# Two attention sublayers on one core: rotation after the query and key units, softmax over two score buffers, head norm by PSUM bank

## The chip, the cores and the metric

The kernel runs on one core of a Trainium2 chip. The metric is the device time of one execution in microseconds (us), as a median of several. The engines named below are TensorE (PE in the profile, with PEld for its weight loads), VectorE (DVE), ScalarE (ACT), GpSimd (POOL) and SyncE (SP, which issues the weight transfers). Each engine works through its own instructions in program order and waits on semaphores for the others. SBUF is the on-chip memory; PSUM is the accumulator memory that TensorE writes, eight banks of 128 x 512 fp32 values, here P[:, 0] to P[:, 7].

## The reference

One block (a mixer of four branches and a mixture of experts), and behind it two layers of three sublayers each, on 256 rows of 1024 values in fp32. The six sublayers are ffn, sparse attention, ffn, ffn, differential attention, ffn. The change touches the two attention sublayers:

```
# sparse: 16 query heads of 64, one shared key and one value head, an indexer of 8 heads
q, k, qi, ki = rope(...)                      # rotates 16 of each 64 columns
score = sum_h w_h * relu(qi_h . ki)           # the 64 best keys of each row are kept
p = softmax(mask(q . k * 64**-0.5));  o = p v
# differential: 8 heads, two query/key sets, values of 128
a = softmax(q1 . k1) - lambda * softmax(q2 . k2)
o = rmsnorm_over_128(a v) * subln_g * (1 - lam_init)
y = o @ w_out                                 # 1024 x 1024, in both
```

Meanwhile the modulation of the second layer, silu(c) @ ada_w[1], is computed: 1024 x 9216 weights, of which nothing else of the sparse sublayer depends.

## The kernel before

Weights stream through `ring`, six slots of 1 MB. SP issues the load for a slot when the unit that lay in it six units earlier is used up. Weights of a projection or an ffn are split into two fp32r parts, `w_hi` (ACT, `high`, L1470) and `w_lo` (DVE, `low`, L1942), and TensorE multiplies three products of these parts. The output projections (`square_out`, L701) and the modulation (`p_ada`, `fill` in `sparse`) take the ring's fp32 weights directly.

An attention sublayer goes through these stages (PE: `sparse` L1302, `differential` L1379; ACT: `a_sparse` L1824, `a_differential` L1859; DVE: `v_sparse` L2551, `v_differential` L2614).

- `project` (L1291): 7 units of 256 columns (sparse) or 12 (differential), each for both halves i of the rows, 14 or 24 tiles; ACT copies each from bank 0 or 1 to `proj` and counts `proj_out`.
- Rotation (`apply_rope`, L2527, DVE, six instructions a call). DVE waits for the last tile, computes two rows of gains (`out_gain`, `in_gain`) ahead of that wait, rotates everything and then marks `roped`. In the differential sublayer it also waits for an exponential on ACT (`lam_exp`), which stands behind the last copy of `project`.
- `turns` (L1280): PE waits for `roped`, then transposes `proj` in groups of four blocks through banks 2 and 3, and ACT copies each group to `qT`, `kT` or `qiT` (`turned`, L1799).
- In the sparse sublayer the indexer (16 small score tiles, a weighted sum on DVE, and the choice of the 64 best by eight rounds of max and replace), with 36 modulation units given out between the steps of PE by `fill`.
- The softmax loop, n = 0 to 7: row half i = n // 4, heads in four groups hg = n % 4; i = 0 has 128 keys, i = 1 has 256. `scores(n)` writes four score tiles into banks 0 and 1. On DVE `probs_rows` (L2540) waits for them, scales and masks them into the one buffer `big`, takes the row maxima and negates them, then waits for ACT's four exponentials (`softmax_exps`, L1806) and takes the reciprocals; the probabilities go to `pr`. PE transposes `pr` (banks 2, 3), ACT copies that to `pT`, and PE multiplies with the values. PE issues `scores(n+1)` ahead of its wait for the probabilities of n.
- In the differential sublayer the outputs of the eight heads stay in banks 4 to 7. Behind the loop ACT squares all four banks in one instruction, PE sums the squares over each head's 128 values with a matrix of ones into banks 0 to 3, ACT takes Ln and Exp of 128 x 2048 values, and DVE multiplies all in one instruction into `oT`.
- `square_out` writes banks 4 to 7; near its end the first half of the next sublayer's normalized rows is transposed (`turn_normed`, L678) into banks 2 and 3. `turnover` (ACT L1759, DVE L2480) holds the row norms, the residual and the next pre-norm.

## Time and profile before

| | us |
|---|---|
| median of 3 runs (2267.04 to 2272.16) | 2269.96 |
| the profiled execution: its time | 2268.83 |
| its span (first to last instruction) | 2267.1 |

Positions in the trace are us from the start of the span. The sparse sublayer's projection ends at about 1308, its output projection starts at 1424; in the differential sublayer it is 1937 and 2029. A row of the timeline has the start, the busy time, the engine, the line, the operation with its shapes and count, and in brackets how long the engine had been idle and what released it. A fp32 matmul shows as two instructions. TensorE's clock has two levels, 1.2 and 2.4 GHz; the profile gives it as a mean granted clock, 0.50 and 1.00 for the two.

### The profile page before, as it was taken

The page shows a single profiled execution, that of the slowest core. Times are in us where ns is not written, and L with a number is a line of the kernel's source. Part 1 is how long each engine was busy: PE and PEld are TensorE (multiplying, and loading weights), DVE is VectorE, ACT ScalarE, POOL GpSimd, SP SyncE. Part 2 cuts the span into 40 slices and gives each one's busy share as a digit, 9 for nine tenths or more (in the row PEclk, how much of TensorE's full clock was granted, in tenths as well). Part 3 has the DMA queues.
Part 4 walks back from the last instruction along what each step waited for, and adds up shares of the span by engine and source line. Part 5 has one row for each costly group of instructions (what it writes and reads, how often), then busy time and mean ns, then how long its engine had stood idle before and what let it go on. Part 6 is the DMA issues. An engine that isn't in the chain of part 4 may idle for free.

```text
span 2267.1 us, 29656 instructions
## 1 busy us (share of the span) xinstructions
PE 2102.3 (93%) x12013; PEld 1752.0 (77%) x12013; DVE 1189.9 (52%) x1691; ACT 889.3 (39%) x1277; POOL 61.0 (3%) x144
## 2 busy tenths in 40 slices
PE   8999989989899999997999967899999999559998
PEld 6777778778478877876999922599989999437998
DVE  2060352431278888887645554355565554334554
ACT  1233411111156677674433424343343434334333
POOL 5000000000000000000000000000000000000000
PEclk9999986979989999998999998899999999669999
DMA  7875230304689898895555698355546565103562
GB/s 226 286 244 184 75 112 1 112 1 149 264 325 339 295 339 315 299 346 189 178 193 167 205 368 319 112 186 183 188 150 218 172 202 187 56 9 122 186 197 100
DMA packets 207240, 441.81 MB, mean 195 GB/s; under 512 B 8108, under 2 KB 158732, under 8 KB 183584
## 3 DMA queue, kind: packets, MB, share of 16 engines
q1 hardware_dynamic: 201568, 424.70, 54.0%
q0 software_dynamic: 5568, 15.67, 2.1%
q8 instruction: 72, 1.18, 0.2%
q14 instruction: 32, 0.26, 0.0%
HBM read 439.14 MB, written 1.20 MB: 194 GB/s over the span
## 4 chain that ended last, share of the span: by engine, by line
PE 66%; DVE 7%; ACT 4%; DMA 2%; issue 1%; DVEq 0%; ACTq 0%
PE P L659 65%; ACT big L1445 1%; DMA ring<-in_ada_w 1%; DMA ring<-in_w_up 1%; ACT merged L1445 1%; DVE w_lo L1950 1%; DVE h L1903 1%; DVE w_lo L2342 1%; DVE xs L1903 1%; PE P L1288 0%; DVE big L1903 0%; DVE st L2546 0%; DVE big L1896 0%; PE P L1179 0%; ACT pT L1445 0%
## 5 line engine op out<-in xcount | busy, mean ns | idle before, releaser
L1950 DVE TENSOR_TENSOR w_lo<-ring,w_hi 128x1024 fp32r<-128x1024 f32 x302 | 351.6, 1220 | 93.0 <-ACT w_hi L1477 92.9
L659 PE MATMUL P<-x_hi,w_hi 128*128 128x256 f32 x1280 | 360.3, 282 | 2.1 <-DVE w_lo L1950 2.1
L659 PE MATMUL P<-x_hi,w_lo 128*128 128x256 f32 x1280 | 361.2, 282 | 0.0
L659 PE MATMUL P<-x_lo,w_hi 128*128 128x256 f32 x1280 | 358.3, 280 | 0.0
L1477 ACT ACTIVATE w_hi<-ring 128x1024 fp32r<-128x1024 f32 x302 | 297.6, 1050 | 65.9 <-DMA ring<-in_ffn_w_down 62.6
L2342 DVE TENSOR_TENSOR w_lo<-ring,w_hi 128x1024 fp32r<-128x1024 f32 x240 | 278.8, 1221 | 18.6 <-ACT w_hi L1670 16.7
L1670 ACT ACTIVATE w_hi<-ring 128x1024 fp32r<-128x1024 f32 x240 | 240.3, 1052 | 95.8 <-DMA ring<-in_w_up 39.8
L659 PE MATMUL P<-xT,ring 128*128 128x256 f32 x1152 | 266.6, 388 | 4.5 <-ACT xT L1445 3.1
L659 PEld LDWEIGHTS P<-xT,ring 128*128 128x128 f32 x1152 | 222.0, 195 | 50.5 <-issue 20.2
L659 PEld LDWEIGHTS P<-x_hi,w_hi 128*128 128x128 f32 x1280 | 240.8, 188 | 6.1 <-DVE w_lo L1950 2.8
L659 PEld LDWEIGHTS P<-x_lo,w_hi 128*128 128x128 f32 x1280 | 242.4, 189 | 2.8
L659 PE MATMUL P<-w_hi,x_hi 128*128 128x256 f32 (+2 forms) x752 | 242.3, 341 | 1.7 <-DVE w_lo L2342 1.7
L659 PEld LDWEIGHTS P<-x_hi,w_lo 128*128 128x128 f32 x1280 | 241.7, 189 | 0.0
L659 PE MATMUL P<-w_lo,x_hi 128*128 128x256 f32 (+2 forms) x752 | 238.7, 338 | 0.0
L659 PE MATMUL P<-w_hi,hid_hi 128*128 128x512 f32 x512 | 202.7, 396 | 1.7 <-DVE hid_lo L1896 1.4
L659 PE MATMUL P<-w_lo,hid_hi 128*128 128x512 f32 x512 | 204.1, 399 | 0.0
L659 PE MATMUL P<-w_hi,hid_lo 128*128 128x512 f32 x512 | 200.7, 392 | 0.0
L659 PE MATMUL P<-w_hi,x_lo 128*128 128x256 f32 (+2 forms) x752 | 186.7, 330 | 0.0
L1661 ACT ACTIVATE silu<-P 128x256 f32<-128x256 f32 x88 | 33.9, 385 | 371.4 <-PE P L659 352.5
L2327 DVE TENSOR_TENSOR hid<-silu,P 128x256 f32<-128x256 f32 (+1 forms) x80 | 33.7, 421 | 251.1 <-ACT silu L1661 250.2
L659 PEld LDWEIGHTS P<-w_hi,x_hi 128*128 128x128 f32 x752 | 148.8, 198 | 16.8 <-issue 2.6
L659 PEld LDWEIGHTS P<-w_lo,x_hi 128*128 128x128 f32 x752 | 146.8, 195 | 12.9 <-issue 0.5
(432 smaller groups left out, 2492.1 us busy)
## 6 DMA issues: line engine op xcount, KB each, us to landing
ring<-in_ada_w SPq DMA_DIRECT2D x72, 1024.0 KB, 9.0
ring<-in_ffn_w_gate SPq DMA_DIRECT2D x44, 1024.0 KB, 5.5
ring<-in_ffn_w_up SPq DMA_DIRECT2D x44, 1024.0 KB, 8.0
ring<-in_ffn_w_down SPq DMA_DIRECT2D x44, 1024.0 KB, 4.9
ring<-in_w_in SPq DMA_DIRECT2D x40, 1024.0 KB, 7.4
ring<-in_w_gate SPq DMA_DIRECT2D x40, 1024.0 KB, 4.9
ring<-in_w_up SPq DMA_DIRECT2D x40, 1024.0 KB, 4.9
ring<-in_w_down SPq DMA_DIRECT2D x40, 1024.0 KB, 4.9
```

Source lines behind the costliest of these rows:

```text
L659: return pe.matmul(o, l, r, start=start, stop=stop, **kw)
L1445: a.done(act.activation(o, i, fn, **kw), name)
L1477: act.activation(w_hi[:, slot, c:c + half], ring[:, slot, c:c + half], ACT.Copy).then_inc(sem("w_hi"), 1)
L1661: act.activation(silu[:, k % 2, :], P[:, k % 2, 0:S], ACT.Silu).then_inc(sem("silu"), 1)
L1670: act.activation(w_hi[:, n % R, c:c + UNIT // 2], ring[:, n % R, c:c + UNIT // 2], ACT.Copy).then_inc(sem("w_hi"), 1)
L1903: v.done(dve.scalar_tensor_tensor(out=o, in0=x, scalar=s, in1=y, op0=op0, op1=op1), name)
L1950: dve.tensor_tensor(w_lo[:, slot, c:c + half], ring[:, slot, c:c + half], w_hi[:, slot, c:c + half].bitcast(F32), ALU.subtract).then_inc(s ...
L2327: dve.tensor_tensor(x, silu[done:128, k % 2, :], P[done:128, k % 2, S:2 * S], ALU.mult).then_inc(sem("hid_part"), 1)
L2342: dve.tensor_tensor(w_lo[:, n % R, c:c + UNIT // 2], ring[:, n % R, c:c + UNIT // 2], w_hi[:, n % R, c:c + UNIT // 2].bitcast(F32), ALU.su ...
```

## The change

- Rotation. The sparse sublayer rotates queries and keys (c0 = 0, 17 heads) after tile 10 of the projection, marks `roped`, and rotates the indexer's part after tile 14, with a second mark; PE and ACT turn all query blocks first, then wait for the second mark and turn the indexer's. The differential sublayer rotates after tile 16 (units 0 to 7 hold queries and keys), then splits its last unit (`low` of unit 11), then does the lambda and the two gain rows, which both stood ahead of the rotation.
- Two score buffers. `bigs` is `big` and a part of `merged`; the row statistics alternate between st[24:32] and st[32:40]. `probs_rows` is cut into `masked_rows(n)` and `row_parts(n)`. DVE does masked_rows(n+1) ahead of row_parts(n), ACT the exponentials of n+1 ahead of the copy of n's transposes, and PE issues scores(n+2) ahead of its wait for n. The rotation's scratch moves from `big` to the other half of `merged`.
- Head norm by bank. ACT waits for `o_psum` in every iteration, and for i = 1 squares that bank (128 x 512) at once. PE sums the first three banks in iteration 7, ahead of its transposes, ACT takes their Ln ahead of the last copy to `pT` and their Exp behind it; the fourth follows behind the loop, its sum issued between the first and second weight unit of `square_out`. DVE normalizes bank by bank, and `square_out` waits for each before the unit that needs it.
- Banks. The differential sublayer's `square_out` writes banks 0 to 3 (`out_bank`), and the turned rows of the next sublayer go to 4 to 7 (`turn_bank`).

```diff
+        bigs = big, acc[:, 0, :].rearrange("p (a b) -> p a b", b=S)
+        def out_bank(n):
+            return 0 if SUBLAYERS[n] == "differential" else 4
+        def turn_bank(n):
+            return 4 if n and SUBLAYERS[n - 1] == "differential" else 2
...
-            def square_out(lhs, name, turn_first):
+            def square_out(lhs, name, turn_first, bank=4, ahead=lambda u: None):
...
                 for u in range(2):
+                    ahead(u)
...
                 for u in (2, 3):
+                    ahead(u)
...
 # PE, sparse
                 for i in range(2):
                     turns([proj[:, i, 128 * k:128 * k + 128] for k in range(8)])
+                t.see("roped")
+                for i in range(2):
                     turns([proj[:, i, 1152 + 128 * k:1280 + 128 * k] for k in range(4)])
                 fill(5)
...
 # PE, sparse and differential
                 scores(0)
+                scores(1)
                 for n, (i, hg) in enumerate(units):
-                    if n + 1 < len(units):
-                        scores(n + 1)
+                    if n + 2 < len(units):
+                        scores(n + 2)
 # PE, differential
+                def head_sums(hg, bank):
+                    t.see("squares")
+                    t.tell(mm(P[:, bank, :], ones[:, :], sq_o[:, hg * 512:hg * 512 + 512]), "square_sums")
...
+                    if n == 7:
+                        pe.wait_ge(sem("s_read"), base_s + 8)
+                        for k in range(2):
+                            head_sums(k, k)
+                        head_sums(2, 2 + (t.sent["pt"] + 1) % 2)
                     t.see("p_ready")
...
-                t.see("squares")
-                for b in range(4):
-                    x = mm(P[:, b, :], ones[:, :], sq_o[:, b * 512:b * 512 + 512])
-                t.tell(x, "square_sums")
-                t.see("o_normed")
+                def ahead(u):
+                    if u == 1:
+                        head_sums(3, 4)
+                    t.see("o_normed")
...
 # ACT, differential (the sparse one has the same order of exponentials)
+                def head_roots(hg, fn):
+                    o = sq_o[:, hg * 512:hg * 512 + 512]
+                    if fn == ACT.Ln:
+                        a.see("square_sums")
+                        bank = (0, 1, 2 + (a.sent["pt_out"] + 1) % 2, 4)[hg]
+                        f(o, P[:, bank, :], ACT.Ln, scale=1 / 128, bias=eps_ln[:, 1:2])
+                    else:
+                        f(o, o, ACT.Exp, "o_rs", scale=-0.5)
+                softmax_exps(0, 0)
                 for n in range(8):
                     i, hg = n // 4, n % 4
-                    softmax_exps(n, i)
+                    if n < 7:
+                        softmax_exps(n + 1, (n + 1) // 4)
+                    else:
+                        for k in range(3):
+                            head_roots(k, ACT.Ln)
                     a.see("pt")
...
-                a.see("o_psum", 8)
-                f(sq_o[:, :], P[:, 4:8, :].rearrange("p a b -> p (a b)"), ACT.Square, "squares")
-                a.see("square_sums")
-                rsqrt(sq_o[:, :], P[:, 0:4, :].rearrange("p a b -> p (a b)"), 1 / 128, eps_ln[:, 1:2], "o_rs")
+                    if n == 7:
+                        for k in range(3):
+                            head_roots(k, ACT.Exp)
+                    a.see("o_psum")
+                    if i:
+                        f(sq_o[:, hg * 512:hg * 512 + 512], P[:, 4 + hg, :], ACT.Square, "squares")
+                head_roots(3, ACT.Ln)
+                head_roots(3, ACT.Exp)
...
 # DVE, sparse
                 low(unit[0], range(2, len(SPARSE_WIDTHS)))
-                out_gain(n, "sparse")
-                in_gain(n + 1)
+                dve.wait_ge(sem("proj_out"), proj_before[0] + 10)
+                for i in range(2):
+                    apply_rope(i, 0, 17)
+                v.mark("roped")
                 dve.wait_ge(sem("proj_out"), proj_before[0] + 14)
                 for i in range(2):
-                    apply_rope(i, 0, 17)
                     apply_rope(i, 1152, 9)
                 v.mark("roped")
 ... (the eight copies to dup)
+                out_gain(sub, "sparse")
+                in_gain(sub + 1)
 # DVE, differential
-                low(unit[0], range(2, DIFF_IN // 256))
-                out_gain(n, "differential")
-                in_gain(n + 1)
+                low(unit[0], range(2, DIFF_IN // 256 - 1))
+                dve.wait_ge(sem("proj_out"), proj_before[0] + 16)
+                for i in range(2):
+                    apply_rope(i, 0, 32)
+                v.mark("roped")
+                low(unit[0], (DIFF_IN // 256 - 1,))
 ... (lambda)
+                out_gain(sub, "differential")
+                in_gain(sub + 1)
                 dve.wait_ge(sem("proj_out"), proj_before[0] + 24)
-                for i in range(2):
-                    apply_rope(i, 0, 32)
-                v.mark("roped")
...
+                masked_rows(0, 0, mask[0])
                 for n in range(8):
-                    probs_rows(i, keep[:, 1, 128:256] if i == 0 else keep[:, 1, :])
-                    ts(st[:, 29:32:2], st[:, 29:32:2], st[:, 58:59])
+                    if n < 7:
+                        masked_rows(n + 1, (n + 1) // 4, mask[(n + 1) // 4])
+                    big_n, c = row_parts(n)
+                    ts(st[:, c + 1:c + 4:2], st[:, c + 1:c + 4:2], st[:, 58:59])
...
-                v.see("o_rs")
-                stt(oT[:, :, :].rearrange("p a b -> p (a b)"), sq_o[:, :], st[:, 59:60], P[:, 4:8, :].rearrange("p a b -> p (a b)"),
-                    ALU.mult, ALU.mult, "o_normed")
+                for hg in range(4):
+                    v.see("o_rs")
+                    stt(oT[:, 2 * hg:2 * hg + 2, :].rearrange("p a b -> p (a b)"), sq_o[:, hg * 512:hg * 512 + 512], st[:, 59:60],
+                        P[:, 4 + hg, :], ALU.mult, ALU.mult, "o_normed")
```

## Rows read from the trace of the kernel before

**Rows 1.** The page, parts 1 and 2 (slices of 56.7 us).
```profile
PE 2102.3 (93%) x12013; PEld 1752.0 (77%) x12013; DVE 1189.9 (52%) x1691; ACT 889.3 (39%) x1277; POOL 61.0 (3%) x144
...
PE   8999989989899999997999967899999999559998
```

**Rows 2.** Windows: from:to, length, busy us (count) by engine, clock, DMA share, GB/s.
```profile
1320.00:1322.00 2.00, 2.00 (x21) 0.83 (x24) 0.00 (x0) 1.20 (x2) 0.00 (x0) 1.00 0.00 0
...
1340.00:1342.00 2.00, 0.00 (x0) 0.00 (x0) 1.79 (x7) 0.00 (x0) 0.00 (x0) 1.00 0.98 410
...
1957.00:2012.00 55.00, 30.25 (x120) 21.26 (x120) 30.30 (x70) 20.37 (x68) 0.00 (x0) 0.53 0.00 0
```

**Rows 3.** Timeline, sparse sublayer, end of the projection: PE.
```profile
1307.74 2.76 PE L659 MATMUL P<-ring,cols 128*1 128x512 f32 x24
1315.65 3.51 PE L1288 MATMUL P<-ident,proj 128*128 128x128 f32 x16 [5.15 <-DVEq L226]
...
1320.59 4.47 PE L659 MATMUL P<-ring,cols 128*1 128x512 f32 x40
```

**Rows 4.** Timeline of PE, sparse softmax loop, and the start of its output projection.
```profile
1364.66 1.23 PE L659 MATMUL P<-kT,qT 64*128 64x128 f32 x8
...
1373.48 1.90 PE L659 MATMUL P<-ring,cols 128*1 128x512 f32 x16
1376.57 0.66 PE L1362 MATMUL P<-ident,pr 128*128 128x128 f32 x4 [1.19 <-DVE pr L1896]
1377.97 0.65 PE L659 MATMUL P<-pT,proj 128*64 128x256 f32 x4 [0.75 <-ACT pT L1445]
1378.55 0.71 PE L659 MATMUL P<-kT,qT 64*128 64x128 f32 x8
...
1424.47 27.69 PE L659 MATMUL P<-ring,oT 128*128 128x512 f32 x60 [1.22 <-ACT oT L1445]
```

**Rows 5.** Timeline, differential sublayer: end of the projection, rotation, first transposes.
```profile
1937.74 1.28 ACT L1445 ACT_TABLE_LOAD   x1
...
1939.72 1.80 DVE L1896 TENSOR_TENSOR big<-proj,rope 128x256 f32<-128x256 f32 x4
...
1945.31 5.34 PE L1288 MATMUL P<-ident,proj 128*128 128x128 f32 x24 [8.16 <-DVEq L226]
...
1953.79 0.69 DVE L1903 SCALAR_TENSOR_TENSOR big<-P,keep 128x512 f32<-128x512 f32 x1 [7.94 <-PE P L659]
```

**Rows 6.** Timeline, differential softmax loop: an iteration with 128 keys, one with 256.
```profile
1957.67 0.18 DVE L1909 RECIPROCAL st<-st 128x4 f32<-128x4 f32 x1 [2.27 <-ACT big L1445]
...
1960.81 1.22 PE L659 MATMUL P<-pT,proj 128*128 128x128 f32 x4 [0.53 <-ACT pT L1445]
...
1993.49 0.60 ACT L1445 ACTIVATE pT<-P 128x512 f32<-128x512 f32 x1 [3.63 <-PE P L1412]
...
1994.14 2.08 PE L659 MATMUL P<-pT,proj 128*128 128x128 f32 x8 [0.75 <-ACT pT L1445]
...
1997.63 0.18 DVE L1909 RECIPROCAL st<-st 128x4 f32<-128x4 f32 x1 [2.69 <-ACT big L1445]
...
1999.92 1.22 DVE L1903 SCALAR_TENSOR_TENSOR big<-P,keep 128x1024 f32<-128x1024 f32 x1
```

**Rows 7.** Timeline, differential sublayer, from the last value product to the output projection.
```profile
2009.48 2.08 PE L659 MATMUL P<-pT,proj 128*128 128x128 f32 x8 [0.75 <-ACT pT L1445]
2011.65 1.88 ACT L1445 ACTIVATE h<-P 128x2048 f32<-128x2048 f32 x1 [2.22 <-PE P L659]
...
2013.58 6.08 PE L659 MATMUL P<-h,ones 128*128 128x512 f32 x8 [2.03 <-ACT h L1445]
...
2021.04 1.97 ACT L1445 ACTIVATE h<-P,eps_ln 128x2048 f32<-128x2048 f32 x1
...
2026.33 2.35 DVE L1903 SCALAR_TENSOR_TENSOR oT<-h,st,P 128x2048 f32<-128x2048 f32 x1 [18.58 <-ACT h L1445]
...
2028.73 27.65 PE L659 MATMUL P<-ring,oT 128*128 128x512 f32 x60 [9.07 <-DVE oT L1903]
```

More of the change, by code:

```diff
@@ L686, in turn_normed @@
                         c = (4 * b + k) * 128
-                        mm(P[:, 2 + 2 * i + b, k * 128:k * 128 + 128], pre_shift[:, c:c + 128], ones[0:1, :], start=k == 0, stop=False,
+                        mm(P[:, turn_bank(n) + 2 * i + b, k * 128:k * 128 + 128], pre_shift[:, c:c + 128], ones[0:1, :], start=k == 0, stop=False,
                            skip_group_check=True)
@@ L1422, in differential @@
                     t.tell(x, "o_psum")
-                t.see("squares")
-                for b in range(4):
-                    x = mm(P[:, b, :], ones[:, :], sq_o[:, b * 512:b * 512 + 512])
-                t.tell(x, "square_sums")
-                t.see("o_normed")
-                square_out(lambda k, i: oT[:, k, i * 128:i * 128 + 128], "out", lambda: turn_normed(sub + 1, 0))
+                def ahead(u):
+                    if u == 1:
+                        head_sums(3, 4)
+                    t.see("o_normed")
+                square_out(lambda k, i: oT[:, k, i * 128:i * 128 + 128], "out", lambda: turn_normed(sub + 1, 0), out_bank(sub), ahead)
             t.see("consts")
@@ L1752, in out_squares @@
                 one, two = st[:, 12 + i:13 + i], st[:, 14 + i:15 + i]
-                f(acc[:, i, 0:512], P[:, 4 + 2 * i, :], ACT.Square, "row_rs", accum_out=one)
+                f(acc[:, i, 0:512], P[:, out_bank(n) + 2 * i, :], ACT.Square, "row_rs", accum_out=one)
                 f(one, one, ACT.Identity, scale=1 / D, bias=eps_ln[:, 1:2])
                 a.see("row")
-                f(acc[:, i, 512:D], P[:, 5 + 2 * i, :], ACT.Square, accum_out=two)
+                f(acc[:, i, 512:D], P[:, out_bank(n) + 1 + 2 * i, :], ACT.Square, accum_out=two)
                 f(st[:, 16 + i:17 + i], two, ACT.Sqrt, "row_rs", scale=1 / D, bias=one)
@@ L2530, in apply_rope @@
                 x1, x2 = x[:, :, 0:8], x[:, :, 8:16]
-                w = [big[:, k, 0:8 * heads].rearrange("p (h d) -> p h d", d=8) for k in range(4)]
+                w = [acc[:, 1, k * S:k * S + 8 * heads].rearrange("p (h d) -> p h d", d=8) for k in range(4)]
                 sin, cos = over(rope[:, i, 0, :], heads), over(rope[:, i, 1, :], heads)
@@ L2599, in v_sparse @@
                     tt(keep[:, i, d0:d0 + 128], keep[:, i, d0:d0 + 128], causal_neg[:, :], ALU.add)
+                masked_rows(0, 0, keep[:, 0, 0:128])
                 for n in range(8):
```

95 lines of the change are left out of this document (54 added, 41 removed).

## The prediction

> **What bounds the kernel now.** I read the page first. TensorE is busy for 93% of the span, so over most of it only less matrix work would help. The slices of the page [rows 1] show where that doesn't hold: four slices at 6, 7, 5 and 5 tenths. By the timeline the first pair is the sparse sublayer (TensorE's work from the end of its projection, 1307.74 [rows 3], to its output projection, 1424.47 [rows 4]: 117 us), the second the differential one (last projection copy about 1937.7 [rows 5], output projection 2028.73 [rows 7]: 91 us). The change edits only these stretches. The ffns and the experts keep their instructions, and each sublayer hands over to the next by `square_out` and the same turnover, so what is gained ahead of `square_out` should arrive whole at the end.
>
> Then the timeline of each stretch, for what ends each wait. In the loop of the differential sublayer the engines take turns: DVE idles 2.69 us for ACT's exponentials, ACT 3.63 us for PE's transposes, and TensorE, with 30.25 us busy of 55, sits at a mean clock of 0.53, nearly always its lower level of 1.2 GHz [rows 2, 6]. It is a chain of latencies, not a full engine. Behind it is the head norm: four large steps one after another, in which TensorE waits 9.07 us [rows 7]. In the sparse sublayer there is a second limit, the modulation's weights: between its waits the DMA engines run at a share of 0.98 with 410 GB/s, so a 1.05 MB unit takes about 2.5 us, but from 1320 to 1322 they carry nothing [rows 2], because PE stood 5.15 us waiting for the rotation and gave no slot back [rows 3].
>
> **Part 1, rotation in the sparse sublayer.** PE ends its first three modulation units at 1310.5 and transposes from 1315.65 [rows 3]. With queries rotated inside the projection (DVE is idle there) the transposes start at 1310.5; the indexer's part of the rotation, about 3.1 us behind the last projection copy near 1308.3, ends while the four query groups are being turned. `fill(5)` starts at about 1315 instead of 1320.6: 5 to 6 us earlier for PE. But up to `scores(0)` at 1364.66 [rows 4] the stretch is paced by the weight stream. The stream can win only the time in which it stood still: the empty window of 2 us and parts of its neighbours, which I estimate at 3.4 us in all. I take 3.4; bounds 0 (the next wait takes it over) and 5.6 (PE's gain arrives whole). The gain rows move behind the copies to `dup`, 2.5 us in which DVE otherwise waits for the first indexer tile; cost 0, and 2.5 if that cover goes.
>
> **Part 2, sparse loop.** From `scores(0)` to `square_out` it is 59.8 us now, 5.7 for an iteration with 128 keys (the score tiles .71, two units 1.90, a wait for DVE of 1.19, transposes .66, the copy .75, values .65 [rows 4], less some overlap). With exponentials one iteration ahead the wait for the probabilities goes: PE's own chain is .71 + 1.90 + .66 + .75 + .65 = 4.67, against 5.0 for two units of the stream; but the stream has a lead of units in the ring at that point, so 4.65 holds for these few. The lead-in (two score tiles, two maskings, first exponentials) makes the first iteration about 10.3. With 256 keys ACT becomes the longest: exponentials 2.6 and two copies of .6 [rows 6], the product with the values, twice the .65, the copy to `oT` .4: 5.4. Now 59.8 less four of 5.7 leaves 36.9 for four of these with lead-in and end, some 8 each. Sum 10.3 + 14.4 (three narrow ones, the last with wider score tiles) + 21.9 = 46.6, gain 13.2. Bounds: 6, if the low clock stretches PE's share (eight score instructions show 1.23 at 1364.66 and .71 at 1378.55 [rows 4]), 15 if DVE's 4.2 us an iteration were the limit. I take 12.6, and with part 1 16 for the sublayer. The ring's last units land at about 1389 and the four of `w_out` by 1400 at 2.5 us each, ahead of a `square_out` at 1408.
>
> **Part 3, rotation in the differential sublayer.** The rotation of 5.6 us, and the 8.16 us that TensorE idles for it [rows 5], go inside the projection: it starts at tile 16 and ends at about 1920. Queued behind it on DVE is the split of unit 11, ready then at about 1922.5; PE takes that unit at 1931.4. That cover of 9 us hides it; without it the cost is up to 5.6. ACT still does its table load and lambda first, until 1939.25, and then has eight groups to copy. The transposes of such a group took .89 (5.34 / 6), partly at the low clock [rows 5]; I estimate .7 a group, since TensorE comes busy from the projection: first masking at 1945.95 instead of 1953.79 [rows 5], gain 7.8. The lambda and gain rows (1939.3 to 1943) fit on DVE ahead of it.
>
> **Part 4, differential loop.** The new order leaves ACT a chain in one iteration: wait for the value product of n, square .6, exponentials of n+2 2.6, copy .6, product 2.08 [rows 6, 7] plus .1 of hand-over each: 6.05 with 256 keys at the low clock (PE's own chain, scores 2.0, transposes 1.1, copy .7, product 2.08, is as long), 5.0 at the high clock, where DVE's 4.97 meets it. Now it is 7.67: masking 2.69 (1.22, as long again for the maxima, and the negation), the wait of 2.69, and 2.29 from the reciprocal at 1997.63 to the next masking at 1999.92 [rows 6]. With 128 keys: exponentials 2.27, copy .45, product 1.22 [rows 6], 3.95, against 5.8. First masking to the end of the value product of n = 6: 8.4 for n = 0 (maskings 1.7, exponentials 2.3, parts 1.9, transposes .7, copy .45, product 1.25), then 3.95 x 2, 4.25, 5.4, 6.05 x 2 = 38.0, so 1983.95.
>
> **Part 5, head norm.** Now from the end of the last product, 2011.56, to `square_out` 17.2 us [rows 7]. After: at 1983.95 PE does three sums (6.08 for four, at mostly the low clock; I count 1.7 each, 5.1), transposes 1.1, ACT's copy .7, product 2.1, and behind its start ACT's Exp with a table load (1.28 [rows 5]) and .6 (1.97 / 4 + overhead [rows 7]), DVE's quarter .7: `square_out` at about 1993.8. The fourth bank's sum adds .9 inside it; its Ln and Exp, with two more table loads, run beside the second weight unit and are done 5 us ahead of the fourth. Squares are hidden in the loop. In all 34.9 - .9 = 34.0 at the low clock.
>
> The new loop keeps TensorE busy for about 80% of a low-clock iteration, and the sparse loop with a similar share shows mostly the high level. If the high clock holds throughout, the iterations and sums give 8 more. I take 2 of these: 36; bounds 31 and 42.
>
> On the two extra table switches: the row shows Ln starting 1.30 us after the load began [rows 5, 7], with nothing between. The Trainium skill (ScalarE: Activation LUTs, What ACT_TABLE_LOAD costs) says that every switch also pays a drain of about 1.38 us, 2.66 in all. By that estimate `square_out` would start 1.4 to 2 us later, since the first Ln and Exp stand in the chain; by the row nothing is added, and the sum goes by the row.
>
> **Sum.** 16 + 36 = 52 off the profiled execution's 2268.83 gives 2216.8; the median of the runs lies 1.1 above that execution, so 2218. I say 2217.
>
> **The rivals.**
> A. The clock rises: the differential loop at 2.4 GHz, DVE-bound. 6 more: 2211 and down to 2207. For it: the busy share; against it: 55 us at 0.53 now [rows 2].
> B. The pipeline doesn't overlap: each engine's queue is in order, ACT waits for the value product before it may begin the next exponentials, so both loops keep their periods, and only the rotations (3.4 + 7.8) and the tail (about 14) are won: 25, so 2245. For it: the wait on `o_psum` is new inside the differential loop; against it: the chain above, in which what waits is shorter than what is taken out.
> C. The stream decides in the sparse sublayer: its units come at 2.5 us and its loop gains only 5: 2225. For it: the DMA share; against it: the stream ends long ahead of `square_out`.
> D. Slower. `square_out` starts the stage colder: it is interrupted by the fourth sum and by four waits for DVE, and if TensorE stays at 1.2 GHz through both output projections, each of 27.65 us at mostly the high level [rows 7] takes twice that, 55 more in all, which eats the gain of 52: 2273. It decides from about 50 us of additional low clock. Against it: the wait ahead of `square_out` is shorter than the 9.07 us of now, after which the clock rose within the first few products.
>
> **How the numbers follow.** Forecast .55, A .22, B .09, C .11, D .03. The range 2204 to 2232 holds the forecast, A and C, and leaves B and D out. A measurement of this kernel can tell about 0.2% (4.5 us) from no change: faster .96, within .01, slower .03 by these cases.
>
> **What would show it.** Part 1: PE's transposes at 1310.5, and no empty DMA window near 1320. Part 2: 5.4 us between copies to `oT` for 256 keys. Part 3: PE idle under 3 us behind the projection. Part 4: 6 us between maskings, not 7.67. Part 5: four table loads, `square_out` 10 us behind the seventh product. Wrong if the loops keep their periods, if the projection waits for unit 11, or if the granted clock in the output projections falls.

## The result, and the profile after

| | before | changed |
|---|---|---|
| time, median of the runs on one chip | 2268.5 us (2267.03 to 2272.16, 4 runs) | 2217.58 us (2211.98 to 2221.52, 4 runs) |
| ratio to before | | 0.977 [0.9753, 0.9787] |
| profiled execution, time / span | 2268.83 / 2267.1 us | 2217.1 / 2215.3 us |
| mean granted clock | 0.935 | 0.944 |

The change makes the kernel 51 us faster, and 2217 was forecast. A right sum can hide wrong terms, so the two traces are set against each other stage by stage. A stage ends at an instruction that both kernels have: `fill(3)` in the sparse sublayer (the first three modulation units behind its projection), the first masking, `square_out`, the last copy of the differential projection.

| stage | before | changed | difference | forecast |
|---|---|---|---|---|
| start to `fill(3)` | 1307.74 | 1307.07 | -0.67 | 0 |
| `fill(3)` to first masking, sparse | 58.27 | 54.66 | -3.61 | -3.4 |
| first masking to `square_out`, sparse | 58.46 | 47.18 | -11.28 | -12.6 |
| that to the last projection copy, differential | 512.79 | 510.66 | -2.13 | 0 |
| last projection copy to first masking | 16.53 | 8.36 | -8.17 | -7.8 |
| first masking to `square_out`, differential | 74.94 | 48.51 | -26.43 | -27.1, and -2 for the clock |
| that to the end | 238.37 | 238.86 | +0.49 | +0.9 |

The seven differences sum to -51.8, the difference of the spans.

The page of the changed kernel, parts 1 and 2, against [rows 1]: TensorE's busy time is 14.7 us less for the same 12013 instructions, and the span is 51.8 us shorter. About 37 us of the gain are thus waiting that went away; the other 14.7 are the same instructions taking less time, at a mean clock of 0.944 instead of 0.935. In the sparse sublayer the slices at 6, 7 and 8 tenths are now at 9, 7 and 8 (a slice is 55.4 us now), in the differential one the pair at 5 and 5 is at 8 and 7.
```profile
PE 2087.6 (94%) x12013; PEld 1744.6 (79%) x12013; DVE 1190.4 (54%) x1694; ACT 893.5 (40%) x1288; POOL 61.0 (3%) x144
...
PE   8999989989989999998999997899999999879998
```

Windows of the changed kernel (from:to, length, busy us and count of PE, PEld, DVE, ACT, POOL, clock, DMA share, GB/s), against [rows 2]. The first lies where the DMA engines had stood still: they now run at full share. The second is the differential loop, at a mean clock of 0.59 (0.53 before).
```profile
1320.00:1322.00 2.00, 1.82 (x16) 0.57 (x16) 0.64 (x2) 1.09 (x4) 0.59 (x1) 1.00 1.04 434
...
1928.00:1968.00 40.00, 26.08 (x117) 18.57 (x118) 31.62 (x72) 22.19 (x74) 0.00 (x0) 0.59 0.00 1
```

The timeline of the sparse sublayer's PE (start, us, engine, line, operation, and in brackets the idle time before and who ended it), against [rows 3, 4]. The transposes start right behind the modulation units, without the 5.15 us for DVE. In the loop the transposes no longer wait for the probabilities; the last three value products are 5.44 and 4.86 us apart.
```profile
1307.07 2.75 PE L668 MATMUL P<-ring,cols 128*1 128x512 f32 x24
1309.75 1.09 PE L1299 MATMUL P<-ident,proj 128*128 128x128 f32 x8
...
1313.78 4.77 PE L668 MATMUL P<-ring,cols 128*1 128x512 f32 x40
...
1378.46 0.66 PE L1376 MATMUL P<-ident,pr 128*128 128x128 f32 x4
...
1396.29 1.09 PE L668 MATMUL P<-pT,proj 128*64 128x256 f32 x8 [0.94 <-ACT pT L1471]
...
1401.73 1.09 PE L668 MATMUL P<-pT,proj 128*64 128x256 f32 x8 [1.51 <-ACT pT L1471]
...
1408.91 25.99 PE L668 MATMUL P<-ring,oT 128*128 128x512 f32 x60 [1.22 <-ACT oT L1471]
```

The timeline of the differential sublayer in the changed kernel, against [rows 5 to 7]. The rotation's multiplications lie at 1896.94, inside the projection, and the transposes no longer wait for DVE. Maskings with 256 keys are 6.11 us apart (7.67 before, [rows 6]). Behind the seventh product come the three sums, and `square_out` starts 8.7 us after that product; in the kernel before it started 25.3 us after the seventh product, and 17.2 us after the last.
```profile
1896.94 1.80 DVE L1945 TENSOR_TENSOR merged<-proj,rope 128x256 f32<-128x256 f32 x4 [2.22 <-ACT proj L1471]
...
1922.24 4.09 PE L1299 MATMUL P<-ident,proj 128*128 128x128 f32 x24 [1.90 <-ACT qT L1471]
...
1927.93 0.69 DVE L1952 SCALAR_TENSOR_TENSOR big<-P,keep 128x512 f32<-128x512 f32 x1 [2.69 <-PE P L668]
...
1951.84 1.22 DVE L1952 SCALAR_TENSOR_TENSOR big<-P,keep 128x1024 f32<-128x1024 f32 x1
...
1957.95 1.23 DVE L1952 SCALAR_TENSOR_TENSOR merged<-P,keep 128x1024 f32<-128x1024 f32 x1 [1.13 <-PE P L668]
...
1965.68 2.07 PE L668 MATMUL P<-pT,proj 128*128 128x128 f32 x8 [1.59 <-ACT pT L1471]
...
1967.55 3.81 PE L668 MATMUL P<-h,ones 128*128 128x512 f32 x6
...
1969.54 1.28 ACT L1471 ACT_TABLE_LOAD   x1 [1.09 <-PE P L668]
1970.84 2.13 ACT L1471 ACTIVATE h<-P,eps_ln 128x512 f32<-128x512 f32 x3
...
1973.62 1.28 ACT L1471 ACT_TABLE_LOAD   x1
1973.65 1.16 PE L668 MATMUL P<-pT,proj 128*128 128x128 f32 x8 [1.86 <-ACT pT L1471]
1974.91 1.95 ACT L1471 ACTIVATE h<-h 128x512 f32<-128x512 f32 x3
...
1976.44 8.83 PE L668 MATMUL P<-ring,oT 128*128 128x512 f32 x16 [1.63 <-DVE oT L1952]
1985.11 1.02 PE L668 MATMUL P<-h,ones 128*128 128x512 f32 x2
1985.97 19.05 PE L668 MATMUL P<-ring,oT 128*128 128x512 f32 x44
```

What is not in the sum of the prediction is the fourth stage. It contains the sparse output projection of 60 matmuls, 27.69 us before [rows 4] and 25.99 here. The same instructions take one or the other in kernels that do not differ there (25.99 to 27.69 in the traces of this case), because they begin at one clock level or the other: over their first 2.5 us the granted clock is 1.00 in all five traces with 25.99, and 0.50 to 0.60 in all six with 27.55 to 27.69. `after_again` (below), the changed kernel itself, took 27.55. So the 1.7 us do not come in every execution. Whether the change makes them likelier is open: all three traces with the old sparse loop took 27.6, and of the eight with the new one five took 25.99 and three 27.6.

### The profile page after: what moved, and what is told of

It reads as the page before. It is cut to its first block, busy times and chain, and to the rows that moved or that the text cites. A ratio compares the mean times of both kernels' runs of the same rounds, so it can differ in the third digit from the quotient of the medians.

```text
span 2215.3 us, 29683 instructions
## 1 busy us (share of the span) xinstructions
PE 2087.6 (94%) x12013; PEld 1744.6 (79%) x12013; DVE 1190.4 (54%) x1694; ACT 893.5 (40%) x1288; POOL 61.0 (3%) x144
## 4 chain that ended last, share of the span: by engine, by line
PE 68%; DVE 5%; ACT 3%; DMA 2%; issue 1%; ACTq 0%; DVEq 0%
PE P L668 67%; DMA ring<-in_ada_w 1%; ACT merged L1471 1%; DMA ring<-in_w_up 1%; DVE w_lo L1999 1%; DVE h L1952 1%; DVE w_lo L2391 1%; DVE xs L1952 1%; ACT pT L1471 0%; PE P L1190 0%; DVE y_lo L1945 0%; ACT st L1471 0%; ACT big L1471 0%; ACT w_hi L1696 0%; DVE xs L1945 0%
```

## The experiments

Runs are named by what was edited. All times are beside runs of the kernel before on the same chip. One caution for all of them: the instant of `fill(3)` scatters from 1300.6 to 1312.0 us between kernels whose instructions are the same up to there (the changed kernel, `squares_late`, `busy_pe`, `all_three`). A difference of 5 us between two single times therefore says little, and the stages say more.

My theory was the prediction's: five parts, each with its own term, the differential loop as a chain in which ACT's wait for the value product and PE's own work are equally long. The rivals were that the gain is one of a chain of engines that only moves when all parts are there, that the weight stream sets the sparse sublayer's pace, and that the wait on `o_psum` costs more than it was booked for.

**One part at a time.** Three kernels, each the kernel before with one part of the change.

`only_rot`: the rotation alone (the edit in extracts; the gain rows and the rotation's scratch move with it, as in the change).
```diff
+                t.see("roped")
+                for i in range(2):
...
-                    turned([qT[:, 0:4, r], qT[:, 4:8, r], qiT[:, 0:4, r]])
+                    turned([qT[:, 0:4, r], qT[:, 4:8, r]])
...
+                dve.wait_ge(sem("proj_out"), proj_before[0] + 16)
+                for i in range(2):
+                    apply_rope(i, 0, 32)
+                v.mark("roped")
+                low(unit[0], (DIFF_IN // 256 - 1,))
```


> Before plus the rotation part alone. Theory (parts as forecast): the sparse sublayer wins the 3.4 us in which the weight stream stood still, the differential one 7.8, so 2268.5 - 11 = 2257, ratio 0.995; in the trace scores(0) of the sparse sublayer at about 1361 and its loop as long as before (59.8), first masking of the differential sublayer 11 us earlier in all. Rival (later waits absorb it): scores(0) stays at 1364 and the time at 2265 or above.

Measured: 2258.24 us (2256.9 to 2264.46, 6 runs), ratio 0.9961 [0.9946, 0.9976] to 2270.07. `fill(3)` to the first masking 54.66, last projection copy to the first masking 8.36: the same as in the changed kernel. The loops behind keep their length (58.79 and 75.37). The timeline of this kernel, the first masking of the differential sublayer:
```profile
1942.11 0.69 DVE L1907 SCALAR_TENSOR_TENSOR big<-P,keep 128x512 f32<-128x512 f32 x1 [2.88 <-PE P L659]
```
The masking's wait for PE is 2.88 us where it was 7.94 [rows 5]. Parts 1 and 3 are worth 3.6 and 8.2 by themselves, as the theory had it.

`only_pipe`: the two score buffers and exponentials one iteration ahead, with rotation and head norm as before.
```diff
                 scores(0)
+                scores(1)
...
-                    if n + 1 < len(units):
-                        scores(n + 1)
+                    if n + 2 < len(units):
+                        scores(n + 2)
...
+                softmax_exps(0, 0)
...
-                    softmax_exps(n, i)
+                    if n < 7:
+                        softmax_exps(n + 1, (n + 1) // 4)
```


> Before plus the two score buffers alone (one squaring of all banks and one head norm behind the loop, as before). Theory: the sparse loop from scores(0) to the output projection goes from 59.8 to 47 to 49 us, the differential loop from first masking to the end of the last value product from 57.8 to about 46 (PE's own chain of 5.95 us an iteration with 256 keys at the low clock is the limit, although ACT here doesn't wait for the value product): 2268.5 - 23 = 2245. Rival (ACT's wait for the product is what limits the changed kernel, not PE's chain): without it the iterations with 256 keys fall to the 5.0 us of DVE, 42 in all, 2241.

Measured: 2239.29 us (2234.56 to 2241.74, 4 runs), ratio 0.9873 [0.9858, 0.9888]. This is below both expectations. The sparse loop takes 46.13 (58.46 before), the differential stage 58.84 (74.94). The last value product ends 42.3 us after the first masking; the theory had 46, the rival 42. The timeline of this kernel, the last two value products and `square_out`:
```profile
1972.52 2.07 PE L660 MATMUL P<-pT,proj 128*128 128x128 f32 x8 [0.75 <-ACT pT L1448]
...
1976.19 2.07 PE L660 MATMUL P<-pT,proj 128*128 128x128 f32 x8 [0.75 <-ACT pT L1448]
...
1994.81 29.03 PE L660 MATMUL P<-ring,oT 128*128 128x512 f32 x60 [9.07 <-DVE oT L1910]
```
Without the squares ACT never waits for the value product in the differential loop. The wide iterations (those with 256 keys) come out at 4.97, 6.14 and, once no scores are left, 3.67. The changed kernel's trace has 5.98 and 5.98 for the first two, but a second execution of it (`after_again`, below) has 5.07 and 6.05, and the seventh product ends 38.62 us after the first masking here, against 39.82 and 39.00 there. The pipeline overlaps fully. What had been left out of the 46 is above all that the last iteration has no scores; how much ACT's wait costs can't be read from this run, since two executions of the changed kernel differ by 0.8 us up to there.

`only_head`: the head norm per bank, with the loops' order as before.
```diff
+                    if n == 7:
+                        pe.wait_ge(sem("s_read"), base_s + 8)
+                        for k in range(2):
+                            head_sums(k, k)
+                        head_sums(2, 2 + (t.sent["pt"] + 1) % 2)
...
-                t.see("squares")
-                for b in range(4):
-                    x = mm(P[:, b, :], ones[:, :], sq_o[:, b * 512:b * 512 + 512])
...
+                    a.see("o_psum")
+                    if i:
+                        f(sq_o[:, hg * 512:hg * 512 + 512], P[:, 4 + hg, :], ACT.Square, "squares")
```


> Before plus the head norm by bank alone, on the unpipelined loop. Theory: from the end of the product of n = 6 to the output projection 25.3 us become about 11, but ACT now waits for each value product and squares ahead of the next exponentials, which in the unpipelined loop stands in the chain: 2 us more in each of three iterations with 256 keys and .8 in each of four with 128, 9 in all. Net 5 to 6 off: 2263; the parts don't add up to the whole change. Rival (parts are independent): no loss in the loop, 14 off: 2254.

Measured: 2262.93 us (2258.61 to 2269.43, 12 runs), ratio 0.9971 [0.9959, 0.9983]. The end of the seventh product moves from 49.63 to 56.45 us behind the first masking (+6.8; expected +9), and from there to `square_out` it is 10.1 us instead of 25.3. This kernel's timeline shows the price of the wait on `o_psum` where nothing is queued ahead of it:
```profile
1999.19 2.07 PE L667 MATMUL P<-pT,proj 128*128 128x128 f32 x8 [0.75 <-ACT pT L1466]
...
2001.37 0.60 ACT L1466 ACTIVATE h<-P 128x512 f32<-128x512 f32 x1 [2.22 <-PE P L667]
...
2008.78 2.07 PE L667 MATMUL P<-pT,proj 128*128 128x128 f32 x8 [0.75 <-ACT pT L1466]
```
ACT sits through the product (2.22), then squares, and the exponentials start that much later: 9.6 us from product to product, 7.7 before. Part 5 alone gives back half of what it wins, and is worth its full size only inside part 4's pipeline, where the exponentials of n+1 have already gone ahead.

The three alone gained 11.8, 30.8 and 7.1 us: 49.7 together, the whole change 51. I had expected 39 for that sum. In the stage where two parts meet, they gained 16.1 and 8.35 apart, 26.4 together: 2.0 more together, so the two help each other a little. The rival of a chain that only moves when all is there is refuted.

**The weight stream.** `half_stream` is the changed kernel with half of each modulation unit of the second layer loaded, and only that half multiplied.
```diff
                 src, m, k, p = load
+                if n in marks["ada"] and n > moe:
+                    src, k = src[:, :, 0:k // 2], k // 2
...
+                part = 1 if layer == 0 else 2
+                w = take().rearrange("p (m n) -> p m n", n=(2048 if q < 4 else 1024) // part)[:, 0:1 if q < 4 else 2]
```


> The changed kernel with only half of the columns of each modulation unit of the second layer loaded and multiplied (half of that modulation is left out). Theory (the weight stream paces the sparse sublayer up to scores(0)): the waits for ring<-in_ada_w go, first masking about 10 us earlier (1351 to 1352 instead of 1361.73), by then paced by the 64-best choice on DVE. Rival (DVE's chain is the limit already): first masking within 3 us of 1361.7. The softmax loop behind it shortens by what PE's units take, 3 to 6 us more.

Measured (one execution): 2210.99 us. `fill(3)` to the first masking 45.4, 9.2 less than the 54.66 of the changed kernel, as expected. TensorE's waits for these units fall from 8.0 to 1.6 us there, the mean granted clock of the stretch rises from 0.81 to 0.92, and at its end DVE masks as soon as its choice of the 64 best is done. First masking to `square_out` 46.97 against 47.18: the expectation of 3 to 6 less there was a miss. The timeline of ACT in this kernel, the copies of the value products to `oT`:
```profile
1395.16 0.38 ACT L1474 ACTIVATE oT<-P 128x256 f32<-128x256 f32 x1 [1.26 <-PE P L670]
...
1400.59 0.38 ACT L1474 ACTIVATE oT<-P 128x256 f32<-128x256 f32 x1 [1.26 <-PE P L670]
```
5.43 us apart, and in the changed kernel, with the full stream, the same:
```profile
1397.50 0.38 ACT L1471 ACTIVATE oT<-P 128x256 f32<-128x256 f32 x1 [1.26 <-PE P L668]
...
1402.93 0.38 ACT L1471 ACTIVATE oT<-P 128x256 f32<-128x256 f32 x1 [1.26 <-PE P L668]
```
So the stream sets the pace up to the first masking, and not one step further. The miss has its reason in the edit: half of the matmuls of a unit take TensorE as long as all of them. The timeline of PE between two value products with 256 keys in the changed kernel, then the same unit in `half_stream`:
```profile
1390.36 1.09 PE L668 MATMUL P<-pT,proj 128*64 128x256 f32 x8 [1.06 <-ACT pT L1471]
1391.38 1.13 PE L668 MATMUL P<-kT,qT 64*128 64x256 f32 x8
1392.44 1.88 PE L668 MATMUL P<-ring,cols 128*1 128x512 f32 x8
1394.26 1.09 PE L1376 MATMUL P<-ident,pr 128*128 128x128 f32 x8
```
```profile
1390.11 1.88 PE L670 MATMUL P<-ring,cols 128*1 128x512 f32 x4
```
Eight instructions take 1.88 us, and four take 1.88 us. So the run halves the bytes and leaves TensorE's time as it was: it tests the stream alone, and says nothing of what a shorter unit would give. It matters, because TensorE is the limit in part of this loop. From this product to the next (1396.29) it is 5.93 us, in which it waits for nothing but the copy of its own transposes (0.94). Only the interval behind that, where no scores are left, is ACT's, with the 5.43 shown above.

Up to the first masking the stream is what limited part 1: PE's transposes and `fill(5)` came 6.1 us earlier behind `fill(3)` (6.71 against 12.85), but only 3.6 us arrived, about the time for which the stream had stood still.

**The wait on `o_psum` and the clock.** In the trace of the changed kernel two chains of about 6 us stand side by side in the differential loop: ACT's (wait for the product, square, exponentials, copy) and PE's own (scores, transposes, copy, product at 1.2 GHz). Two edits take them one at a time.

`squares_late`: ACT squares product n-1 behind the copy of iteration n, so that it never waits for the product just started.
```diff
-                    a.see("o_psum")
-                    if i:
-                        f(sq_o[:, hg * 512:hg * 512 + 512], P[:, 4 + hg, :], ACT.Square, "squares")
+                    elif n:
+                        squared(n - 1)
+                squared(7)
```


> The changed kernel; ACT sees the value product of n and squares its bank one iteration later, behind the copy of n+1, so that it never waits for PE inside the loop. Theory (PE's chain of scores, transposes, copy and product at the low clock is nearly as long, as the kernel with the two buffers alone showed: 38.6 us from first masking to the end of the product of n = 6, against 39.8): 1.2 us off, first masking to output projection from 48.5 to 47.3. Rival (ACT's wait is the limit): the iterations with 256 keys fall from 5.98 to 5.0, 3 us off, 45.5.

Measured (one execution): 2216.49 us; the differential stage 45.89, against 48.51 and 47.69 in two executions of the changed kernel, and 47.68 in `half_stream`, whose differential sublayer is the same. Theory 47.3, rival 45.5: nearer the rival. The timeline and the window of this kernel's loop:
```profile
1962.82 0.60 ACT L1471 ACTIVATE h<-P 128x512 f32<-128x512 f32 x1
1962.84 1.16 PE L668 MATMUL P<-pT,proj 128*128 128x128 f32 x8 [0.75 <-ACT pT L1471]
```
```profile
1932.70:1972.00 39.30, 24.55 (x120) 17.22 (x121) 31.70 (x72) 22.92 (x75) 0.00 (x0) 0.74 0.00 1
```
ACT squares the older product while PE runs the new one, so there is no idle time ahead of it. The seventh product ends 37.44 us after the first masking, against 39.82 and 39.00, and the clock over the loop is 0.74 (0.59 and 0.68). One wide product takes 1.16 us, not 2.07, as one does in `after_again`. That less waiting of ACT also lifts the clock, so that the theory's split into "ACT's wait" and "the clock" was too neat, fits these numbers; with one execution of this kernel, and 0.59 and 0.68 for the same instructions, it is not shown.

`busy_pe`: PE keeps its order and gets matmuls without use into the waits.
```diff
+                def idle(count, ahead=1):
+
+                    for _ in range(count):
+                        mm(P[:, 2 + (t.sent["pt"] + ahead) % 2, 0:S], ident[:, :], ones256[:, :])
...
                 scores(0)
+                idle(2)
                 scores(1)
+                idle(2)
...
                         scores(n + 2)
+                        idle(3)
...
+                    if n < 7:
+                        idle(1, 0)
```


> The changed kernel with extra matmuls of ones into an idle bank in the differential softmax loop (three of 256 columns ahead of PE's wait for the probabilities, one ahead of its wait for the copy, two ahead of scores(1) and (2)); they compute nothing that is used. Theory (the loop is held by the low clock of TensorE, 0.59 mean): with PE busy throughout the granted clock stays near 1.00, a value product with 256 keys takes 1.16 instead of 2.07, the iteration goes to the 5.0 of DVE, the three sums to 2.6; first masking to output projection from 48.5 to 43. Rival (the clock is not what holds it, or the extra work stands in the way): 48.5 or up to 5 longer.

Measured (one execution): the stage 45.2 us, where 43 was expected. (The time, 2207.55, came from a `fill(3)` at 1300.6, 6.5 us earlier than in the changed kernel; this part of it is scatter.) The windows of this kernel: the whole loop, and 10 us inside it.
```profile
1921.70:1958.20 36.50, 31.20 (x175) 22.67 (x176) 31.70 (x72) 22.05 (x73) 0.00 (x0) 0.93 0.00 1
1933.70:1943.70 10.00, 9.56 (x52) 6.66 (x50) 9.28 (x20) 6.03 (x22) 0.00 (x0) 1.00 0.00 0
```
And its timeline, value products with 256 keys:
```profile
1945.68 1.16 PE L668 MATMUL P<-pT,proj 128*128 128x128 f32 x8 [0.31 <-ACT pT L1481]
...
1950.75 1.16 PE L668 MATMUL P<-pT,proj 128*128 128x128 f32 x8 [0.37 <-ACT pT L1481]
...
1954.30 1.11 PE L1445 MATMUL P<-ident,pr 128*128 128x128 f32 x4 [2.40 <-DVE pr L1962]
...
1956.16 2.07 PE L668 MATMUL P<-pT,proj 128*128 128x128 f32 x8
```
At clock 1.00 the products are 5.07 us apart, and DVE is busy for 9.28 of 10 us: at 2.4 GHz it is DVE that limits the loop, as the prediction's 4.97 said. Then the scores end, PE waits 2.40 us for DVE with nothing in the gap, and the next product is at the lower level again (2.07). The wide products from there on are 6.3 and 7.1 us apart, which is where the 2 us lie by which the expectation missed. The Trainium skill (TensorE: Matmul & The Clock Gate, HAM oscillation — how this bites in real kernels) describes a loop that waits for DMA in every round and is thrown back to the lower clock by each wait. The waits here are for other engines and short, at most 1.91 us in the loop of the changed kernel's trace and 2.68 in that of `after_again`, but the outcome agrees: 0.59 and 0.68 with these waits, 0.93 with most of them filled.

**All of it.** `all_three` joins the late squares and the filled waits with Exp's table load inside the projection:
```diff
                         project_out(sub, k)
+                    if k == 12 and units > 7:
+                        table(ACT.Exp)
```


> The changed kernel with the late squares, the extra matmuls, and ACT's table for Exp loaded during the differential projection (behind its 12th copy) instead of behind it. Theory: the table takes 1.28 off the way to the first masking, the other two together 6 (DVE then holds the loop at 5.0 an iteration): 7 off, 2210 to 2211. Rival (extra matmuls cost as much as the clock gives): 2216 to 2218.

`after_again` is the changed kernel once more, beside it on the same chip.

> The changed kernel itself on the chip of these runs: 2217 to 2218, as the measure for the three others. If it lies by more than 2 us elsewhere, differences are taken against this run.

Measured: `all_three` 2215.4 us (2209.15 to 2218.61, 5 runs), ratio 0.9765 [0.974, 0.9789]; `after_again` 2218.84 (2210.47 to 2222.33, 5 runs), ratio 0.9772 [0.9746, 0.9798]. The table load is as the theory had it: last projection copy to the first masking 7.08 instead of 8.36, its 1.28 us exactly. The other two edits are not: the differential stage is 44.04 instead of 47.69, 3.65 us where 6 were expected. By the stages that is 4.9 us of the expected 7, and the time of 2215.4 lies by the rival's 2216 more than by the theory's 2211; the ratios of the two kernels overlap, so by the time of the whole they are not told apart.

`after_again` repeats the differences of the change with other scatter: sparse loop 44.96, differential stage 47.69. Windows of the ten us behind the first sparse masking, in `after_again` first, then in the changed kernel's first execution:
```profile
1364.56:1374.56 10.00, 7.27 (x67) 3.18 (x68) 8.01 (x17) 6.92 (x26) 0.29 (x1) 0.98 1.01 420
```
```profile
1361.73:1371.73 10.00, 7.63 (x48) 3.40 (x48) 6.38 (x13) 4.97 (x19) 0.29 (x1) 0.64 1.02 423
```
The same instructions at 0.98 get 67 matmuls done, at 0.64 only 48. The 2.2 us between the two executions of this stage lie here, in the lead-in.

`all_five` adds two edits: eight more filling matmuls at n = 6, and in the sparse loop the copy to `oT` one iteration later.
```diff
+                    elif n == 6:
+                        idle(8)
...
-                    a.see("o_psum")
-                    f(oT[:, 2 * hg:2 * hg + 2, i * 128:i * 128 + 128],
-                      P[:, 4 + n % 2, 0:S].rearrange("p (a b) -> p a b", b=128), ACT.Copy, "o_out")
+                    for m in (n - 1, n) if n == 7 else (n - 1,) if n else ():
+                        a.see("o_psum")
+                        f(oT[:, 2 * (m % 4):2 * (m % 4) + 2, m // 4 * 128:m // 4 * 128 + 128],
+                          P[:, 4 + m % 2, 0:S].rearrange("p (a b) -> p a b", b=128), ACT.Copy, "o_out")
```


> The kernel with late squares, extra matmuls and early table, plus two edits: eight more extra matmuls at n = 6 of the differential loop, where PE stood 2.4 us at most with the clock falling, and in the sparse loop ACT's copy to oT one iteration later, so that it never waits for the product. Theory: the three sums take 2.6 instead of 3.8 and the last products 1.16 instead of 2.07, first masking to output projection in the differential sublayer 41 to 42 instead of 44.0; in the sparse sublayer PE's chain (5.4 to 5.9 an iteration with 256 keys) is nearly as long as ACT's, so 47.2 falls to 46 at the lowest. About 3 off all_three, 2212, ratio 0.975. Rival for the sparse part (ACT's wait is the limit, since halving PE's units left that loop at 47.0): 256-key iterations go to 4.9, 44.5 us.

One premise of it is wrong: `half_stream` had halved the matmuls of PE's units and not their time, as shown above.

Measured: 2210.79 us (2204.01 to 2214.61, 6 runs), ratio 0.9747 [0.9722, 0.9773]. That is about the 2212 expected, and the lowest ratio of all, though its interval touches that of the changed kernel (0.977 [0.9753, 0.9787]). The differential stage is 43.77, only 0.3 below `all_three`, where 41 to 42 was expected: a miss. The window shows that the clock did what was wanted, the timeline where it went:
```profile
1925.00:1960.00 35.00, 31.42 (x186) 22.86 (x187) 29.37 (x67) 21.93 (x72) 0.25 (x1) 1.00 0.03 10
```
```profile
1963.64 2.74 PE L668 MATMUL P<-h,ones 128*128 128x512 f32 x6
...
1964.75 1.28 ACT L1483 ACT_TABLE_LOAD   x1 [0.25 <-PE P L668]
1966.04 2.12 ACT L1483 ACTIVATE h<-P,eps_ln 128x512 f32<-128x512 f32 x3
1968.20 0.60 ACT L1483 ACTIVATE pT<-P 128x512 f32<-128x512 f32 x1
...
1968.85 1.16 PE L668 MATMUL P<-pT,proj 128*128 128x128 f32 x8 [2.03 <-ACT pT L1483]
```
The three sums now take 2.74 us instead of 3.81, but the last product waits 2.03 us for the copy `pT`, which stands behind the table load and three Ln in ACT's queue. The tail is ACT's there, and a faster TensorE gains nothing. In the sparse loop the value products are at 4.87 us instead of 5.44 in one interval of three, and the stage is 46.74 against 47.18 at a similar lead-in: 0.4. The interval of 5.93 stays, which is TensorE's, so the rival (4.9 for every interval) is out.

## Why the prediction was right

The likeliest case came true, and its terms hold, with three that were mis-sized and cancelled one another.

- **Part 1** (3.4): 3.61, and 3.6 in `only_rot`. The choice between 0 and 5.6 was right for the reason given: `half_stream` shows that the stream paces this stretch.
- **Part 2** (12.6): 11.28 in one execution, 13.5 in the other. The narrow iterations were right, 4.45 to 4.88 between value products with 128 keys for 4.65. The wide ones were priced by the wrong engine: ACT's 5.4 holds for one of the three intervals between products with 256 keys (5.44), while in the first TensorE's own chain of scores, unit, transposes and product needs 5.93, and the last takes 4.86. The four wide iterations with the end, 21.9 in the forecast, took 23.5: 22.3 to the end of the last product, and 1.2 for its copy to `oT` and the hand-over to `square_out`. And one term has two values, the lead-in, which I had put at 10.3 us: up to the end of the first value product it took 10.8 at a clock of 0.64 and 8.6 at 0.98. The low clock that I had feared for the lower bound is there, for 2 us and not for 7.
- **Part 3** (7.8): 8.17, alone and in the whole. The transposes came sooner than estimated (24 in 4.09 us, .68 a group), and the split of the last unit did stay covered: in the last 6 us of the projection PE is busy for 6.00.
- **Part 4** (product n = 6 ends at 38.0): 39.82. The first four products end at 20.7, for 20.55, and the iteration of 6.05 was measured at 5.98 (twice), in the second execution at 5.07 and 6.05. The mis-sized term is the first wide iteration: 7.15 for 5.4. DVE masks a wide tile and takes its maxima before it gets to the probabilities, a round of 5.06 us already, and the product behind is 2.07 instead of .71. The reason given for the 6.05 was half of the truth. Two chains of equal length were said to meet. Without ACT's wait the stage is quicker by 1.8 to 2.6 us (`squares_late`, one execution), where an equally long chain of PE at a clock that stays would have allowed next to nothing. The likely reading, argued and not shown, is that the chains share the clock: a wait taken from ACT shortens PE's idle time, the clock is higher (0.74), and PE's chain is no longer 6 us.
- **Part 5** (9.85 from that product to `square_out`): 8.7, because the sums took 3.81 us for the 5.1 forecast, and the last product 1.16 for 2.1, at 2.4 GHz. With part 4: 34.1 for the differential sublayer in all, as the 34.0 before any bonus for the clock.
- **The clock** (2 of 8 possible): the differential loop was at 0.59, so the 2 did not come there. In their place came 2.1 from the fourth stage, 1.7 of it the sparse output projection at the higher level, which no step of the prediction had named and which `after_again` did not get. The sum was right partly by that luck.
- **The sums.** Three terms don't quite follow from their parts: 59.8 less four of 5.7 is 37.0, not 36.9; the parts of n = 0 add to 8.3, not 8.4; and ACT's chain adds to 5.9 us ahead of its hand-overs, of which the 6.05 counts fewer than four. None moves the forecast by more than 0.3 us an iteration.
- **The extra table switches**: in the tail Ln starts 1.30 us after its load began (1969.54, 1970.84) and Exp 1.29 (1973.62, 1974.91). The later start of 1.4 to 2 us, by the Trainium skill's drain (ScalarE: Activation LUTs, What ACT_TABLE_LOAD costs), is not there: `square_out` came 1.15 us sooner than the sum, not later.

Of the rivals, A (the loop rises to 2.4 GHz by itself) did not occur, but `busy_pe` and `all_five` made it occur, and the loop was then DVE's, as A said. B is refuted by the changed kernel itself: with ACT's wait on `o_psum` in the loop the seventh product ends 39.82 us after the first masking, 49.63 before. `only_pipe` says the same of the sparse loop, 12.3 us shorter. C holds up to the first masking and no further (`half_stream`). D is refuted by the changed kernel itself: its second output projection takes 8.83 + 19.05, against 27.65 [rows 7], with the fourth sum in between.

One expectation behind the prediction also failed: that the parts would gain 39 us separately. They gained 49.7. I had overpriced the wait on `o_psum` in `only_head` (+9, measured +6.8) and underpriced the pipeline without it.

Open: why `fill(3)` scatters by 11 us, what makes an output projection start at one clock level or the other, and how the gain of the late squares divides between ACT's wait and the clock. No run settles these.

## What to carry to other kernels

Where several engines take turns in a loop and TensorE mostly waits, price the new loop by each engine's queue in order, with its waits, at both clock levels, and then say which engine limits at which level; the waits and the clock feed each other, so that they are not to be summed as independent gains. Where the start of a stage scatters more than the effect, compare the lengths of stages between instructions that both kernels have. Once a chain is shortened, look at what stands ahead of its last link in another engine's queue: here the copy behind a table load and three Ln took back what a faster TensorE had given.

## What was not expected of the hardware

- Matmuls of no use, put into TensorE's waits, raised the granted clock of a loop from 0.59 and 0.68 to 0.93 (`busy_pe`), 0.95 (`all_three`) and 1.00 (`all_five`, up to its last two products), and a value product from 2.07 to 1.16 us. With the late squares this gave 3.7 us of the stage's 47.7.
- The granted clock of the same stretch differs between executions of one kernel: 0.59 and 0.68 in the differential loop, 0.64 and 0.98 behind the first sparse masking, and 25.99 or 27.6 us for the same 60 matmuls. Single executions differ by 2 us a stage for that alone.
- With half of each modulation unit's bytes the stretch paced by the stream became 9.2 us shorter, but the loop right behind it, at a DMA share of 1.02 in its first 10 us in the changed kernel, hardly at all (46.97 against 47.18): a full share says that transfers run, not that anybody waits for them.
- The matmuls of a modulation unit have one row of result each and write it to rows 0, 32, 64 or 96 of a bank. With half of them, and of the rows, left out a unit took TensorE as long: 1.04 us with eight instructions and 1.03 with four where there are four such rows, 1.88 and 1.88 where there are two, all at a clock of 1.00. It looks as if matmuls to different ones of these rows run side by side.
